# Third feed-forward of a two-block transformer kernel: down units with tokens on partitions, last norm summed along rows

## The reference

```python
sh1, sc1, g1, sh2, sc2, g2 = [m[:, None, :] for m in jnp.split(mod, N_MOD, axis=-1)]
x = x + g1 * rms_norm(y, mix_post_g[i])
h = rms_norm(x, ffn_pre_g[i]) * (1.0 + sc2) + sh2
g, u = jnp.split(h @ w_ffn_in, 2, axis=-1)
y = (jax.nn.silu(g) * u) @ w_ffn_out
x = x + g2 * rms_norm(y, ffn_post_g[i])
```

## Time and profile before

| what | value |
|---|---|
| median of 3 runs | 1225.48 us (1223.29 to 1226.95) |
| the profiled execution | 1226.85 us, span 1225.1 us, mean granted clock of the matrix engine 0.98 |
| matrix engine busy | 1167.2 us, 95% of the span |
| VectorE busy | 845.8 us, 69% |
| ScalarE busy | 614.6 us, 50% |
| DMA | 214.15 MB, 175 GB/s on average |

### The profile page before, as it was taken

How to read it: one execution, slowest core, us unless ns; L and a number is a source line. 1 busy time by engine, 2 the same in 40 slices (tenths; PEclk the granted TensorE clock), 3 DMA queues, 4 the chain that set the end, 5 groups by cost and what they waited for, 6 DMA issues and landing times.

```text
span 1225.1 us, 21103 instructions
## 1 busy us (share of the span) xinstructions
PE 1167.2 (95%) x9014; PEld 1131.6 (92%) x9014; DVE 845.8 (69%) x1270; ACT 614.6 (50%) x738; POOL 0.2 (0%) x4
## 2 busy tenths in 40 slices
PE   5999999999999999999999999999899988999996
PEld 4799899999999988898999999999899988999996
DVE  6995575777676797964747776767899647644543
ACT  7675336553433464763374644344568465434333
POOL 0000000000000000000000000000000000000000
PEclk9999999999999998999999999999989998999998
DMA  9455342656687553554326657776644232655501
GB/s 347 146 166 179 131 138 74 234 193 218 229 290 277 190 200 102 171 173 138 119 88 207 207 182 265 259 254 222 212 137 138 69 130 70 215 173 191 187 35 35
DMA packets 177614, 214.15 MB, mean 175 GB/s; under 512 B 3696, under 2 KB 160752, under 8 KB 177520
## 3 DMA queue, kind: packets, MB, share of 16 engines
q1 hardware_dynamic: 176800, 211.86, 52.3%
q10 hardware_dynamic: 720, 0.94, 0.2%
HBM read 211.74 MB, written 1.05 MB: 174 GB/s over the span
## 4 chain that ended last, share of the span: by engine, by line
PE 73%; DVE 16%; ACT 6%; issue 2%; DMA 1%; SPq 0%; DVEq 0%; ACTq 0%
PE stream L494 16%; PE stream L496 16%; PE stream L495 16%; DVE w_lo L1346 6%; PE steps L494 5%; PE steps L496 5%; PE steps L495 5%; ACT w_hi L915 3%; PE steps L829 2%; PE steps L684 1%; PE stream L705 1%; DMA raw<-in_w_in 1%; DVE score L1483 1%; PE steps L674 1%; DVE top L1481 1%
## 5 line engine op out<-in xcount | busy, mean ns | idle before, releaser
L1346 DVE TENSOR_TENSOR w_lo<-raw,w_hi 128x2048 fp32r<-128x2048 f32 (+2 forms) x178 | 402.4, 2265 | 230.9 <-ACT w_hi L915 230.0
L915 ACT ACTIVATE w_hi<-raw 128x2048 fp32r<-128x2048 f32 (+2 forms) x178 | 336.5, 1894 | 338.4 <-PE stream L496 302.3
L494 PE MATMUL stream<-h_hi,w_hi 128*128 128x256 f32 x1576 | 451.8, 287 | 7.5 <-DVE h_lo L1738 3.8
L495 PE MATMUL stream<-h_lo,w_hi 128*128 128x256 f32 x1576 | 448.4, 285 | 0.0
L496 PE MATMUL stream<-h_hi,w_lo 128*128 128x256 f32 x1576 | 448.4, 285 | 0.0
L494 PEld LDWEIGHTS stream<-h_hi,w_hi 128*128 128x128 f32 x1576 | 304.8, 193 | 10.2 <-DVE w_lo L1346 5.3
L495 PEld LDWEIGHTS stream<-h_lo,w_hi 128*128 128x128 f32 x1576 | 304.7, 193 | 0.6 <-issue 0.5
L496 PEld LDWEIGHTS stream<-h_hi,w_lo 128*128 128x128 f32 x1576 | 304.6, 193 | 0.0
L494 PE MATMUL steps<-gu_hi,w_hi 128*128 128x256 f32 x528 | 149.6, 283 | 1.9 <-DVE gu_lo L1606 1.9
L495 PE MATMUL steps<-gu_lo,w_hi 128*128 128x256 f32 x528 | 149.4, 283 | 0.0
L496 PE MATMUL steps<-gu_hi,w_lo 128*128 128x256 f32 x528 | 149.4, 283 | 0.0
(11 more groups left out here) (288 smaller groups left out, 1634.7 us busy)
## 6 DMA issues: line engine op xcount, KB each, us to landing
raw<-in_w_ffn_in SPq DMA_DIRECT2D x66, 1024.0 KB, 5.2
raw<-in_w_in SPq DMA_DIRECT2D x54, 1024.0 KB, 5.6
raw<-in_w_ffn_out SPq DMA_DIRECT2D x33, 1024.0 KB, 7.7
ada_raw<-in_ada_w SPq DMA_DIRECT2D x24, 1024.0 KB, 5.3
raw<-in_w_out SPq DMA_DIRECT2D x8, 1024.0 KB, 5.1
raw<-in_w_proj_attn SPq DMA_DIRECT2D x8, 512.0 KB, 3.5
raw<-in_w_proj_hgrn SPq DMA_DIRECT2D x8, 512.0 KB, 4.6
raw<-in_w_o SPq DMA_DIRECT2D x4, 1024.0 KB, 4.9
```

The source lines that it names most:

```text
L494: pe.matmul(dst, w_h, x_h, start=start, stop=False, skip_group_check=True)
L495: pe.matmul(dst, w_h, x_l, start=False, stop=False, skip_group_check=True)
L915: return act.activation(out_, in_, func, **kw)
L1346: tt(wl[m % SPL][:, 0:n], raw[m % RAW][:, 0:n], wh[m % SPL][:, 0:n].bitcast(F32), ALU.subtract)\
```

## The change

- The down units of the third feed-forward have the products stationary (128 tokens at a time) and the weights moving, 512 output features per matmul: 4 quarters (2 token blocks x 2 feature halves) x 2 inner blocks x 3 = 24 matmuls. The accumulators then hold tokens on partitions.
- x is needed in that form too: 16 transposes of 128x128 blocks of `xT` into the fourth stream accumulator, in four calls (`turn_x`) between units of steps 2 to 6, and four copies by ScalarE into `x_tm`. That accumulator is taken out of the rotation for the gate and up units from step 1 on.
- The gain, until now one number per partition, must lie along rows: ScalarE scales the identity by each of eight gain columns (`gain_diag`), ahead of the third mixer's output norm; the matrix engine multiplies the eight by ones (`gain_rows`), after that norm's sum; ScalarE copies both rows out (`gain_evac`), after the second and third pair.
- The last norm: ScalarE squares each quarter and sums it along the row in one operation, the two halves of a token block are joined through the bias of the logarithm (`out_rstd`); its table load comes first. VectorE multiplies a quarter by the gain row (`gained_out`), then by the root and adds x (`finished`). The sum over partitions, the fold and the copies to `y2` fall away at the end (the norm after the mixer keeps them).
- SP stores four pieces of 128 tokens by 512 features in the output's own layout, [256, 1024].

```diff
 def plan_banks():
 ...
+        if u[:3] == ("gate", 2, 1):
+            TURN_FREE.append(last[3])
 ...
             for _ in range(2 if u[0] in ("merge", "tw") or shifted(u) else 1):
+                if bank == 3 and u[0] in ("gate", "up") and u[1] == 2 and u[2] >= 1:
+                    bank = 0
                 banks.append(bank)
 ...
             sp.wait_ge(*x2_new.at(1, j))
-            sp.dma_start(out.rearrange("(c p) t -> p c t", p=P)[:, 2 * j:2 * j + 2, :],
-                         xT[:, 2 * j:2 * j + 2, :]).then_inc(out_done, 16)
+            sp.dma_start(out[P * (j // 2):P * (j // 2) + P, 512 * (j % 2):512 * (j % 2) + 512], x_tm[:, j, :])\
+                .then_inc(out_done, 16)
 ...
+                elif kind == "down" and b == 2:
+                    g_h, g_l = gu_h[name % 2], gu_l[name % 2]
+                    pe.wait_ge(*f_lo.at(b, name))
+                    for j in range(4):
+                        ts, ws = slice(P * (j // 2), P * (j // 2) + P), slice(512 * (j % 2), 512 * (j % 2) + 512)
+                        for k in range(2):
+                            mm = three(A[j], g_h[:, k, ts], g_l[:, k, ts], hi[:, k, ws], lo[:, k, ws], name == 0 and k == 0,
+                                       name == FS - 1 and k == 1)
+                        if name == FS - 1 and j < 3:
+                            mm.then_inc(d_part.sem, 1)
 ...
+        def gain_rows():
+
+            pe.wait_ge(*g_diag.at(0))
+            for c in range(KC):
+                mm = pe.matmul(A[2 + c // 4][:, P * (c % 4):P * (c % 4) + P], ones, gain_diag[:, c, :], start=True, stop=True)
+                if c % 4 == 3:
+                    mm.then_inc(g_row.sem, 1)
+
+        def turn_x(j):
+
+            if j == 0:
+                pe.wait_ge(evac[TURN_FREE[0][0]], TURN_FREE[0][1])
+            else:
+                pe.wait_ge(*x_set.at(0, j - 1))
+            pe.wait_ge(*x2_new.at(0, 3))
+            for c in range(4):
+                mm = pe.transpose(S[3][:, P * c:P * c + P], xT[:, 4 * (j % 2) + c, P * (j // 2):P * (j // 2) + P], ident)
+            mm.then_inc(x_turned.sem, 1)
+
         def feed_forward(b):
 ...
-                stream(3 * FS - 2, normed(5))
+                stream(2, normed(5))
+                pe.wait_ge(*g_set.upto(0))
+                stream(2)
+                for i in range(1, FS - 1):
+                    if 2 <= i < 6:
+                        turn_x(i - 2)
+                    stream(3)
                 return
 ...
         post_sum(0)
+        gain_rows()
         feed_forward(2)
-        post_sum(1)
 ...
+        def gain_evac(i):
+
+            act.wait_ge(*g_row.at(0, i))
+            f(gain_row[:, i, :], A[2 + i], ACT.Copy).then_inc(*lane.mark(g_set))
+
+        def out_rstd():
+
+            ss, rest = den[:, 0, 0:4], den[:, 1, 0:2]
+            act.preload_act_table_set("natural_log_exp_and_others")
+            for j in range(4):
+                t = j // 2
+                act.wait_ge(*(d_part.at(2, j) if j < 3 else (unit_done, len(UNITS))))
+                f(hn[:, 2 * j:2 * j + 2, :].rearrange("p c t -> p (c t)"), A[j], ACT.Square, accum_out=ss[:, j:j + 1])\
+                    .then_inc(*lane.mark(o_sq2))
+                act.wait_ge(*lane.last)
+                if j % 2 == 0:
+                    f(rest[:, t:t + 1], ss[:, j:j + 1], ACT.Identity, scale=1.0 / D, bias=eps).then_inc(*lane.step())
+                else:
+                    f(rs_t[:, t:t + 1], ss[:, j:j + 1], ACT.Ln, scale=1.0 / D, bias=rest[:, t:t + 1]).then_inc(*lane.step())
+                    act.wait_ge(*lane.last)
+                    f(rs_t[:, t:t + 1], rs_t[:, t:t + 1], ACT.Exp, scale=-0.5).then_inc(*lane.mark(o_rs2))
 ...
                 lane.last = f_hi.at(b, i)
+                if b == 2 and 3 <= i < 7:
+                    act.wait_ge(*x_turned.at(0, i - 3))
+                    f(x_tm[:, i - 3, :], S[3], ACT.Copy).then_inc(*lane.mark(x_set))
                 if i:
                     tick()
 ...
+        act.wait_ge(*gains_set.at(1))
+        for c in range(KC):
+            ins = f(gain_diag[:, c, :], ident, ACT.Copy, scale=gain[:, 3, c:c + 1])
+            ins.then_inc(*(lane.mark(g_diag) if c == KC - 1 else lane.step()))
         post(0, lambda j: (b2(UOUT[2] + j), (unit_done, UOUT[2] + j + 1), (evac["act"], 1)))
-        act.wait_ge(*gains_set.at(1))
         shift_hi(1)
         for j in range(4):
             act.wait_ge(*x2_new.at(0, j))
             gained_hi(5, lambda k: gain[:, 1, k:k + 1], j)
             square(5, j)
+            if j in (1, 2):
+                gain_evac(j - 1)
         tick()
         feed_forward(2)
-        post(1, lambda j: (A[j].rearrange("p (c t) -> p c t", c=2),
-                           d_part.at(2, j) if j < 3 else (unit_done, len(UNITS)), None))
+        out_rstd()
 ...
         feed_forward(2)
-        for j in range(4):
-            fold(j, p_sq.at(1, j), p_fold)
-        post(1, lambda c: gain[:, 3, c:c + 1])
+        dve.wait_ge(*x_set.upto(0))
+
+        def gained_out(j):
+
+            dve.wait_ge(*o_sq2.at(0, j))
+            tt(yg[:, j, :], A[j], gain_row[:, j % 2, :], ALU.mult).then_inc(*lane.step())
+            return lane.last
+
+        def finished(j, gained):
+
+            dve.wait_ge(*o_rs2.at(0, j // 2))
+            dve.wait_ge(*gained)
+            stt(x_tm[:, j, :], yg[:, j, :], rs_t[:, j // 2:j // 2 + 1], x_tm[:, j, :], ALU.mult, ALU.add)\
+                .then_inc(*lane.mark(x2_new))
+
+        parts = [gained_out(j) for j in range(3)]
+        finished(0, parts[0])
+        parts.append(gained_out(3))
+        for j in range(1, 4):
+            finished(j, parts[j])
```

More of the change, by code:

```diff
@@ L149, in evac_engine @@
     return None if kind == "down" or first_half(u) else "act"
+TURN_FREE = []
 def plan_banks():
@@ L255, in build @@
     ytmp = at("y2_term", [P, 2, T], F32, 136)
+    yg = at("y_gained", [P, 4, 512], F32, 128)
+    x_tm = at("x_tm", [P, 4, 512], F32, 144)
+    gain_row = at("gain_row", [P, 2, 512], F32, 152)
+    gain_diag = at("gain_diagonal", [P, KC, P], F32, 160)
     top = [base + 199 * 1024]
@@ L354, in build @@
     x2_new = Event("x2_updated", 4)
+    g_diag, g_row, g_set = Event("gain_diagonals_set"), Event("gain_rows", 2), Event("gain_rows_set", 2)
+    x_turned, x_set, o_sq2, o_rs2 = Event("x_turned", 4), Event("x_tm_set", 4), Event("out_squares", 4), Event("out_rstd", 2)
     ada_out = Event("ada_evacuated")
@@ L627, in post_sum @@
         def post_sum(i):
-            if i:
-                pe.wait_ge(*y_copied.at(0, 0))
             for j in range(4):
@@ L2012 @@
            for k, x in arrays.items()}
-    out = nc.dram_tensor("out", (D, T), F32, kind="ExternalOutput").ap()
+    out = nc.dram_tensor("out", (T, D), F32, kind="ExternalOutput").ap()
     build(nc, aps, out)
     r = run_bass_kernel_spmd(nc, [{"in_" + k: x for k, x in arrays.items()}], core_ids=[0])
-    return np.ascontiguousarray(r.results[0]["out"].T)[None]
+    return np.ascontiguousarray(r.results[0]["out"])[None]
```

## The result

| | before | changed |
|---|---|---|
| median of the runs compared | 1224.44 us (8 runs, 1222.41 to 1226.95) | 1219.88 us (8 runs, 1212.01 to 1220.32) |
| ratio of the times, 95% interval | | 0.9949 (0.9927 to 0.9971) |
| profiled execution: time, span | 1226.85, 1225.1 us | 1219.87, 1218.1 us |
| mixer's last logarithm to first down matmul | 35.69 us | 35.68 us |
| first down matmul to the last quarter ready | 167.30 us (to T0) | 165.71 us |

The account below looks back on a forecast made before the run. The matrix engine bounds the dense third feed-forward; in the tail, a late table load, then VectorE alone. Pace -3.6, turning x +1.8, gain rows 0 and tail -6.5 make -8.3 us: median 1217.2 us, range 1214.8 to 1221.0.

Parts of the forecast that it names:

- T0: In the tail before the change: the worked-out moment, about 1212.18 us, when the last down unit's last quarter is ready.
- Pace: Third feed-forward's down units: 24 matmuls of 512 columns replacing 48 of 256 save 3.6 us over 11 units.
- Rival 2: Down units: 512 columns cost twice 256, so 3.6 us are lost again, giving 1220.8 us; chance 0.06.
- Rival 4: Down units: 512-column matmuls wait for their stationary operands, 43 us more, giving 1260 us; chance 0.03.
- Turning x: Dense third feed-forward stretch: 16 transposes at 0.11 us each add 1.8 us, all on the path.
- rival 3: After each turn of x the clock drops, four falls costing 7.4 us, giving 1224.6 us; chance 0.05.
- Gain rows: Around the third mixer's output norm: diagonals, products and copies fit idle stretches, costing 0; clock gain possible up to 1.85 us.
- Rival 1: Before the first gate: shorter idleness keeps the clock up, 1.85 us less, giving 1215.4 us; chance 0.14.
- The tail: From the last quarter ready to the end: 6.4 us instead of 12.92, 6.5 us saved (6.0 to 7.0).
- The sum: Whole kernel: -3.6 + 1.8 + 0 - 6.5 = -8.3 us, profiled execution 1218.55 us, median 1217.2 us.

## Why the prediction was right

- **Pace**: 3.6 us forecast, 3.3 measured by going back to 256 columns. The pitch was right to 0.0001 us (0.2265); the step of the sum that was a little too large is 24 pitches for a whole unit, since each unit starts some 0.03 us more slowly than that. Rival 2 (no gain) falls by that experiment. Rival 4 falls with the pitch too: it needed 0.258.
- **Turning x**: 1.8 us forecast, 1.76 measured by doubling it, and 0.42 for a single turn taken out of the stream. The clock stays at 1.00 with four and with eight in a row: rival 3 falls. The prediction charged all four as path "because the engine has no gap there"; that holds for the four places chosen, but the gap of 1.21 us just ahead of the first down unit would have taken one.
- **Gain rows**: 0 forecast; 35.68 us against 35.69 from the logarithm to the first down matmul. The cover named, ScalarE's two idle stretches and the matrix engine's gap, is what the rows show. The clock was left at a gain of 0, as forecast. Rival 1 named a true mechanism and the wrong condition: shortening the gap to 3.59 us was not enough; with more work and 0.91 us of idleness the clock stayed up.
- **The tail**: 6.5 us forecast, 6.64 measured in the first profile of the changed kernel and 6.8 to 7.0 with the four others that have this tail (12.92 less 5.95 to 6.14). That the first comes so near is luck in part, since two estimates were off against each other in it. VectorE ended 3.40 us after the last quarter was ready, not 3.75: the read of the sum overlaps the squares and VectorE was through with quarter 0 at 0.71, so the product started at 0.73 rather than 0.94; the next operation started 0.60 behind it instead of 0.69; and three finishing operations take 2.07, 0.69 each, the lower bound. The store took 2.88 instead of 2.63 in that profile, 2.55 to 2.74 in the others. The root is no limit: it was there at 1213.07, and the first operation that needs it is the finishing of quarter 2, the second of the three that run from 1213.15 on, so it starts near 1213.84. With quarter 1 finished earlier that reserve is gone: in that experiment the root is ready at 1211.42 and the finishing of quarter 2 starts at 1211.51. What the working did not ask is whether VectorE's order was the best one: it priced three finishing operations behind the last product, where two are enough. That the product waits those 0.73 us for the squares is still in every version; letting both engines read the quarter at once was not tried.
- **The sum**: 8.3 us forecast and 8.23 found behind the first down matmul. Applied to the profiled execution it gave 1218.55 us; it was 1219.87, the 1.24 us being the part ahead of the logarithm. Applied to the median it gave 1217.2; the two medians of the changed kernel, 1219.88 and 1219.54, lie 2.7 and 2.3 above it, inside the range. That they lie inside is luck: the upper end of the range was made for rival 2, a lost gain in pace, and not for the scatter of the unchanged part. By the time alone rival 2, with its 1220.8 us, would even be nearer than the forecast; only the distances inside the profiles and the experiment with 256 columns decide against it. The step that is too thin is the last one, from one profiled execution to a median: the prediction took off the 1.37 us between the two and put nothing into the range for the executions themselves, when the unchanged part alone spreads by 7.9 us over ten profiles.

## What to carry to other kernels

Where the matrix engine is the limit, wider moving operands pay by the matmuls that disappear, here some 13 ns for each; transposes needed for the new layout are paid at their full length in a dense stream, and at nothing in a gap that is there anyway. When a tail is a chain of two engines, list which operations depend on the last result and move every other one ahead of it, the function table load first. And when the effect is as small as the spread of the unchanged part, cut both traces at the same events and compare the distances: profiles of the same stage agreed there to a few tenths of a microsecond, where whole times lay up to seven apart.

## What the runs showed that was not expected

- Filling the matrix engine's gap with matmuls whose result nobody needs shortened the stage: 12 more of them, 35.68 to 34.21 us, and 34.23 in the second kernel that had them. With sixteen records and 3.59 us of idleness behind them the clock still fell to 0.50, with 40 and 0.91 us it stayed at 1.00.
- The same instructions ahead of the change took between 1002.6 and 1010.4 us in ten profiles, with falls of the granted clock at different places.
- Two operations in a row on one engine overlap in the records: the read of the accumulator starts 0.50 us after squares of 0.60, and three finishing operations of 0.74 us take 2.07 together. Durations added up give a chain that is some tenths too long; starts are the better ruler.
